# Eight dense projections of a two-layer block, joined into two chains of four with hand-placed buffers

## What is computed

```python
for layer in range(2):
    mod = (silu(c) @ ada_w[layer] + ada_b[layer])[:, None, :]
    sh1, sc1, g1, sh2, sc2, g2 = split(mod, 6)
    hh = rms_norm(x, norm1_g[layer]) * (1 + sc1) + sh1
    mix = nsa_mixer(hh, ...) if layer == 0 else rglru_mixer(hh, ...)
    x = x + g1 * mix                        # mix ends in @ w_out
    hh = rms_norm(x, norm2_g[layer]) * (1 + sc2) + sh2
    g, u = split(hh @ ffn_w_in[layer], 2)
    x = x + g2 * ((silu(g) * u) @ ffn_w_out[layer])
q, k, v = split(x @ w_qkv, 3)               # first step of the third layer
```

## The kernel before

| name | n, tiles, kt | matmuls | ahead of it | behind it |
|---|---|---|---|---|
| nsa_out | 4, 2, 8 | 192 | sparse attention | x mixed on VectorE |
| ffn0_in | 22, 2, 8 | 1056 | norm | h = silu(g)*u, split |
| ffn0_out | 8, 1, 22 | 528 | | x mixed |
| rg_in | 11, 2, 8 | 528 | norm | convolution, gelu |
| rg_out | 8, 1, 11 | 264 | recurrence | x mixed |
| ffn1_in | 22, 2, 8 | 1056 | norm | h, split |
| ffn1_out | 8, 1, 22 | 528 | | x mixed |
| da_in | 12, 2, 8 | 576 | x split | attention |

## Time and profile before

### The profile page before, as it was taken

How to read it: one execution, slowest core, us unless ns; L and a number is a source line. 1 busy time by engine, 2 the same in 40 slices (tenths; PEclk the granted TensorE clock), 3 DMA queues, 4 the chain that set the end, 5 groups by cost and what they waited for, 6 DMA issues and landing times. The chain is left out here.

```text
span 3203.3 us, 65861 instructions
## 1 busy us (share of the span) xinstructions
PE 2878.2 (90%) x27525; PEld 2113.0 (66%) x27525; DVE 1447.0 (45%) x2538; ACT 884.9 (28%) x1564; POOL 306.9 (10%) x422
## 2 busy tenths in 40 slices
PE   7999999999999999999989996874988899996985
PEld 5766778887856788888756763542567876663652
DVE  5678578533665433322374221212595654221222
ACT  3256332212454222213362000003342343000002
POOL 2125211001200000000000000001121430000001
PEclk9999999999999999999999998997899999998997
DMA  9720167442302333413217899997113217999997
GB/s 288 203 72 2 27 223 239 142 125 63 102 23 64 92 92 104 109 54 114 99 39 327 368 425 427 427 425 299 47 53 88 48 49 302 421 425 427 426 426 293
DMA packets 378757, 638.75 MB, mean 199 GB/s; under 512 B 91380, under 2 KB 328609, under 8 KB 344489
## 3 DMA queue, kind: packets, MB, share of 16 engines
q1 hardware_dynamic: 341497, 560.04, 47.8%
q0 software_dynamic: 15776, 51.63, 4.4%
q10 hardware_dynamic: 21264, 23.88, 2.2%
HBM read 611.06 MB, written 24.38 MB: 198 GB/s over the span
## 5 line engine op out<-in xcount | busy, mean ns | idle before, releaser
L2326 DVE TENSOR_TENSOR moe_scratch<-masks_b,moe_ps 128x128 f32<-128x128 f32 x102 | 39.4, 386 | 637.4 <-ACT masks_b L2183 637.4
L2125 PE MATMUL moe_ps<-moe_ring,moe_scratch 128*32 128x256 f32 x3616 | 233.1, 409 | 84.6 <-DMA moe_ring<-in_moe_w_gu 74.6
L217 PE MATMUL ffn_in_ps<-ffn_xhi,ffn_in_whi 128*128 128x512 f32 x704 | 274.8, 390 | 5.3 <-DVE ffn_xlo L493 4.4
L218 PE MATMUL ffn_in_ps<-ffn_xlo,ffn_in_whi 128*128 128x512 f32 x704 | 274.6, 390 | 0.0
L219 PE MATMUL ffn_in_ps<-ffn_xhi,ffn_in_wlo 128*128 128x512 f32 x704 | 274.5, 390 | 0.0
L2125 PEld LDWEIGHTS moe_ps<-moe_ring,moe_scratch 128*32 128x32 f32 x3616 | 137.4, 116 | 172.4 <-issue 90.3
L2110 PE MATMUL moe_ps<-xT,causal 128*32 128x256 f32 x3296 | 206.7, 389 | 0.0
L2110 PEld LDWEIGHTS moe_ps<-xT,causal 128*32 128x32 f32 x3296 | 127.8, 114 | 59.5 <-issue 10.8
L2183 ACT ACTIVATE masks_b<-moe_ps 128x128 f32<-128x128 f32 x102 | 28.4, 278 | 493.2 <-PE moe_ps L2125 491.2
L217 PEld LDWEIGHTS ffn_in_ps<-ffn_xhi,ffn_in_whi 128*128 128x128 f32 x704 | 132.6, 188 | 34.3 <-issue 5.4
L219 PEld LDWEIGHTS ffn_in_ps<-ffn_xhi,ffn_in_wlo 128*128 128x128 f32 x704 | 132.6, 188 | 27.4
(11 more groups left out here) (843 smaller groups left out, 6089.0 us busy)
## 6 DMA issues: line engine op xcount, KB each, us to landing
moe_ring<-in_moe_w_gu SPq DMA_DIRECT2D x80, 2048.0 KB, 37.7
moe_ring<-in_moe_w_down SPq DMA_DIRECT2D x40, 2048.0 KB, 35.0
da_moe_units<-in_moe_w_gu SPq DMA_DIRECT2D x24, 2048.0 KB, 37.9
rw_AR<-in_moe_w_gu SPq DMA_DIRECT2D x24, 2048.0 KB, 41.0
ffn_came<-in_ffn_w_in SPq DMA_DIRECT2D x88, 512.0 KB, 5.1
da_moe_units<-in_moe_w_down SPq DMA_DIRECT2D x12, 2048.0 KB, 32.5
rw_AR<-in_moe_w_down SPq DMA_DIRECT2D x12, 2048.0 KB, 29.9
ffn_late_lo<-in_ada_w POOLq DMA_DIRECT2D x32, 512.0 KB, 5.7
```

Of the source, the lines that this page charges most:

```text
L217: nc.tensor.matmul(ps[0:width, slot * tiles + o], high, xhi[:, k], start=(k == 0), stop=False)
L218: nc.tensor.matmul(ps[0:width, slot * tiles + o], high, xlo[:, k], start=False, stop=False)
L2125: last = nc.tensor.matmul(psGU[j * BLK:(j + 1) * BLK].rearrange("p (g a n) -> p g a n", g=2, a=2), xbT[:, k], cols[:, j], start=(k == 0), ...
L2326: V.tensor_tensor(h.rearrange("p (a m i) -> p a i m", a=2, m=2), gated.rearrange("p (a i m) -> p a i m", a=2, m=2), psU.rearrange("p (a i ...
```

## The change

The seven calls of `dense` from ffn0_in on and the one for nsa_out are replaced by eight `Dense` objects in two chains: nsa_out, ffn0_in, ffn0_out, rg_in, and rg_out, ffn1_in, ffn1_out, da_in. `run_chain` opens one block for a chain, and each engine runs through its four projections in order, held back by semaphores alone. All loops are written out. All buffers of a chain are put at byte addresses chosen by hand (`placed`), and its PSUM banks are shared (`ChainRoom`), so that the weights of the next projection have a place while the one before still runs.

- At the end of a projection ScalarE and VectorE split the first weight block of the next one (`after.first_high`, `after.first_low`) ahead of taking the last product. ffn_out splits 16 of 22 tiles then and the other six behind the last product. ffn1_in has its second block split ahead too (`second_before`).
- Where a norm follows, its squares are all made on ScalarE, two tiles of x in turn, in the projection ahead, and TensorE sums those of block i-2 ahead of the products of block i. ScalarE loads the table of the root (`warm_root`) there.
- The first block of a projection runs through kt in the outer loop. ffn_out starts when 19 of the 22 tiles of h are made, and waits for the last three singly. nsa_out gives its last block's two tiles to VectorE one by one. da_in splits its first tile of x ahead, the others behind.
- The fillers are (4, 5, 8) in place of (6, 3, 22) for ffn and (3, 3, 16) for rg_in; rg_out's three and da_in's six go, and so do those behind the last block of all but rg_in and da_in (12 and 3).
- `recycle` now runs ahead of nsa_out, between rg_in and the recurrence, and ahead of rg_out, and no longer ahead of ffn0_in and ffn1_in. The loads of ada_w may start when nsa_out's products are done, and `load_band` when ffn0_out's are.

```diff
+    def load(self, sp, i):
+        if i < 2 and self.preloaded[i]:
+            return
+        if i >= 2:
+            sp.wait_ge(self.low_done, self.split_at(i - 2))
+        elif self.before_load:
+            self.before_load(sp, i)
+        for dst, src in self.loads(self.first_raw if i == 0 else self.raw[i % 2], i):
+            sp.dma_start(dst, src).then_inc(self.w_loaded[i % 2], 16)
...
+    def products(self, pe, i):
+        nc = self.B.nc
+        if i == 0:
+            order = [(o, k) for k in range(self.kt) for o in range(self.tiles)]
+        else:
+            pe.wait_ge(self.low_done, self.split_at(i))
+            order = [(o, k) for o in range(self.tiles) for k in range(self.kt)]
...
+                if self.h_made is not None and o == 0 and (k == 0 or k >= self.kt - 3):
+                    pe.wait_ge(self.h_made, max(k + 1, self.kt - 3))
+            out = self.banks[i % 2][:, o]
+            nc.tensor.matmul(out, high, self.xhi[k], start=(k == 0), stop=False)
+            nc.tensor.matmul(out, high, self.xlo[k], start=False, stop=False)
+            last = nc.tensor.matmul(out, low, self.xhi[k], start=False, stop=(k == self.kt - 1))
...
+    def tensor(self, pe, after):
+        norm = after.norm if after else None
+        for i in range(self.n):
+            if norm and i >= 2:
+                norm.sum_tiles(pe, self.tiles_at(i - 2))
+            self.products(pe, i)
+            if self.parts and i == self.parts.fold_after:
+                self.parts.fold(pe)
+        if norm:
+            norm.sum_tiles(pe, self.tiles_at(self.n - 2))
+            stay_busy(self.B, self.unread, after.busy[0])
+            norm.sum_tiles(pe, self.tiles_at(self.n - 1))
+            stay_busy(self.B, self.unread, after.busy[1])
+            norm.spread(pe)
+            stay_busy(self.B, self.unread, after.busy[2])
+        if self.unread_behind:
+            stay_busy(self.B, self.unread, self.unread_behind)
...
+    def scalar(self, act, before, after):
+        norm = after.norm if after else None
+        if self.norm:
+            self.norm.root(act)
+            for k in range(self.kt):
+                self.norm.shift(act, k, self.xhi[k]).then_inc(self.x_hi_done, 1)
+        elif self.x is not None:
+            for k in range(1 if before else 0, self.kt):
+                self.x_high(act, k)
+        if before is None:
+            for q in range(len(self.first_parts)):
+                self.first_high(act, q)
+        for i in range(1, self.n):
+            if not (i == 1 and self.second_before):
+                self.split_high(act, i)
+            if self.act_body:
+                self.take_on_act(act, i - 1)
+            if norm and i >= 2:
+                norm.square_tiles(act, self.tiles_at(i - 2))
+        if after:
+            after.first_high(act, 0)
+            if after.x is not None:
+                after.x_high(act, 0)
+            if after.second_before:
+                after.split_high(act, 1)
+        if norm:
+            norm.square_tiles(act, self.tiles_at(self.n - 2))
+            norm.warm_root(act)
+        if self.act_body:
+            self.take_on_act(act, self.n - 1)
+        if norm:
+            norm.square_tiles(act, self.tiles_at(self.n - 1))
+        if after:
+            for q in range(1, len(after.first_parts)):
+                after.first_high(act, q)
...
+        elif self.x is not None:
+            for k in range(1 if before else 0, self.kt):
+                self.x_low(dve, k)
+        if self.dve_start:
+            self.dve_start(dve)
+        if before is None:
+            for q in range(len(self.first_parts)):
+                self.first_low(dve, q)
+        for i in range(1, self.n):
+            if not (i == 1 and self.second_before):
+                self.split_low(dve, i)
+            if self.parts:
+                self.parts.accumulate(dve, i)
+            if self.dve_body:
+                self.take_on_dve(dve, i - 1)
+        if after:
+            after.first_low(dve, 0)
+            if after.x is not None:
+                after.x_low(dve, 0)
+            if after.second_before:
+                after.split_low(dve, 1)
+        if norm:
+            norm.coefficients(dve)
+        if self.dve_body:
+            self.take_on_dve(dve, self.n - 1)
+        if after:
+            for q in range(1, len(after.first_parts)):
+                after.first_low(dve, q)
...
+    def square_tiles(self, act, tiles):
+        for k in tiles:
+            act.wait_ge(self.x_ready, k + 1)
+            if k >= 2:
+                act.wait_ge(self.summed, k - 1)
+            self.B.nc.scalar.activation(self.sq[:, k % 2], self.B.xT[:, k], self.B.ACT.Square).then_inc(self.squared, 1)
+    def warm_root(self, act):
+        self.B.nc.scalar.activation(self.spare, self.B.eps_rms[:], self.B.ACT.Sqrt)
+    def sum_tiles(self, pe, tiles):
+        for k in tiles:
+            pe.wait_ge(self.squared, k + 1)
+            sum_by_chunk(self.B, self.ps, self.sq[:, k % 2], k).then_inc(self.summed, 1)
...
-            dense(B, f"ffn{layer}_in", KF, 2, KD, P, P, loads, None, busy=(6, 3, 22), after=9, parts=parts, unrolled=parts is not None,
-                  act_body=lambda i, slot, ps: nc.scalar.activation(gated[:, slot], ps[:, 0], ACT.Silu),
-                  dve_body=product, xhi=xhi, xlo=xlo, norm=norm, sp_tail=early.load, slots=in_slots, coming=early)
...
+    first = Dense(B, N + "in", KF, 2, KD, loads, tiles_of(xhi, KD), tiles_of(xlo, KD), (came[:, 0], came[:, 1]), (whi[:, 0], whi[:, 1]), (wlo[:, 0], wlo[:, 1]),
+                  room.pairs, unread=room.unread, norm=norm, busy=(4, 5, 8), parts=parts, second_before=layer == 1,
+                  before_load=(lambda sp, i: sp.wait_ge(before.low_done, 2)) if layer == 1 else None,
+                  before_high=lambda act, i, q: act.wait_ge(before.products_done, before.n) if i == 1 and layer == 0 else None,
+                  before_parts=lambda pool: pool.wait_ge(before.products_done, before.n),
+                  act_body=lambda i, slot, ps: nc.scalar.activation(gated[:, slot], ps[:, 0], ACT.Silu), dve_body=product)
...
+    def out_load(sp, i):
+        if i == 0:
+            sp.wait_ge(first.low_done, first.split_at(KF - 1))
+        else:
+            sp.wait_ge(first.products_done, KF)
+    def out_high(act, i, q):
+        act.wait_ge(first.products_done, KF if i or q else KF - 1)
+    second = Dense(B, N + "out", KD, 1, KF, lambda w, i: [(w, w_out[:, :, i * P:(i + 1) * P])], tiles_of(hhi, KF), tiles_of(hlo, KF),
+                   (raw0[:], raw1[:]), (hi0[:], hi1[:]), (lo0[:], lo1[:]), room.singles, unread=room.unread, first_parts=[(0, 16), (16, KF)],
+                   h_made=h_made, before_load=out_load, before_high=out_high, dve_body=add_mixed(B, layer, 5, 1, x_done))
...
-        dense(B, "nsa_out", 4, 2, KD, P, P, out_loads, None, after=8, dve_body=add_mixed(B, 0, 2), xhi=ohi, xlo=olo, is_split=True, early=early, slots=(out_first[:], early.second[:]))
...
+    B.recycle(keep=[early.loaded, early.second_loaded, early.head_hi, early.head_lo])
+    mixed = [B.sem(f"x_mixed{q}") for q in range(2)]
+    chain_scope = ExitStack()
+    room = ChainRoom(B, "chain0", chain_scope)
+    first = Dense(B, "nsa_out", 4, 2, KD, out_loads, tiles_of(ohi, KD), tiles_of(olo, KD), (out_first[:], early.second[:]), (whi[:, 0], whi[:, 1]), (wlo[:, 0], wlo[:, 1]),
+                  room.pairs, unread=room.unread, early=early, dve_body=add_mixed(B, 0, 2, 2, mixed[0]), last_by_tile=True)
+    feed = ffn(B, 0, room, mixed[0], mixed[1], first)
+    return rg_lru(B, chain_scope, room, [first, *feed], mixed[1])
...
+        last = Dense(B, "rg_in", KR, 2, KD, in_loads, tiles_of(yhi, KD), tiles_of(ylo, KD), (in_came[:], in_second[:]), (high0[:], high1[:]), (low0[:], low1[:]),
+                     room.pairs, unread=room.unread, first_raw=in_first[:], norm=norm, busy=(4, 5, 8), unread_behind=12,
+                     before_load=lambda sp, i: sp.wait_ge(out0.products_done, out0.n) if i else sp.wait_ge(out0.low_done, 2),
+                     before_high=lambda act, i, q: act.wait_ge(out0.products_done, out0.n) if i else None,
+                     dve_start=pad, act_body=take, dve_body=convolve, pool_body=load_band)
+        run_chain(B, [*chain, last])
+        chain_scope.close()
+        B.recycle(keep=[tanhed, gelued, convolved, conv_chain, cubed])
...
+    last = Dense(B, "da_in", 12, 2, KD, qkv_loads(B), [x0[:, 0]] + tiles_of(xhi, KD - 1), [x0[:, 1]] + tiles_of(xlo, KD - 1), (w0[:], w1[:]), (high0[:], high1[:]),
+                 (low0[:], low1[:]), room.turned_pairs, unread=room.unread, first_raw=in_first[:], x=B.xT, x_ready=x_ready,
+                 before_load=lambda sp, i: sp.wait_ge(out1.products_done, out1.n) if i else sp.wait_ge(out1.low_done, 2),
+                 before_high=lambda act, i, q: act.wait_ge(out1.products_done, out1.n) if i else None,
```

(45 more changed lines are left out.)

369 lines of the change are left out of this document (251 added, 118 removed).

## The result

The changed kernel takes 3182.9 us (median of four runs, 3181.35 to 3185.16) where the kernel before took 3206.07 in the same session: a ratio of 0.9925, 95% interval 0.9913 to 0.9937. It is 23.2 us faster, and 3183 was forecast. The sum behind that number did not come out so well, as the traces show.

A forecast was written before the change was run, and what follows sets the result against it. TensorE, busy 90% of the span, was the bound, so only its lost time could go: of 62.1 us 38.5 stay, 23.6 less, span 3203.3 to 3179.7, median 3183 (own range 3177 to 3189; 8 in 10: 3173 to 3194).

The forecast's parts named there:

- The losses before: Joints, slow stretches and waits in the eight projections: 62.1 us lost, the most that the change could take away.
- The joint with a norm: Ahead of ffn0_in, rg_in and ffn1_in: 7.3 us still lost at each, 21.9 in all (bounds 6.8 and 9 each).
- The joints without one: Ahead of ffn0_out and ffn1_out 0.1 us each stays lost, 0.2; at da_in 0.5 (bounds 0.3 and 2).
- The sums that move: 16 tile sums between products of nsa_out, ffn0_out and rg_out: 0.35 us each, 5.6 (bounds 3.9 and 8).
- The second blocks: Waits for the second weight block: ffn0_in keeps its 0.9 us and rg_in gets one, 1.8 together.
- The barriers: Three new ones, ahead of nsa_out, the recurrence and rg_out, cost 5.1 us, covered by no work (bounds 3 and 6).
- The clock: Slow stretches at rg_out's start and the new barriers cost 3.4 us (bounds 0 and 7); none at the norms.
- Loops written out: Writing out the loops of five projections gains and costs nothing.
- the first: Clock falls at the norms all the same, and at new barriers: 16 to 19 us less, 3188 to 3191; chance 0.17.
- the second: Weight split ahead holds up the queue, five joints lose 2 to 3 us each: 3194 to 3198; chance 0.08.
- the fourth: TensorE starves for instructions in 50 newly written-out blocks: slower, 3233 at 1 us a block; chance 0.05.
- The third: More gained: sums hidden behind products, barriers covered, no slow stretch at all: 3171 to 3176; chance 0.09.

The follow-up runs named there:

- the weights behind the root: Changed kernel with first weight blocks of ffn0_in, rg_in and ffn1_in split behind root and reciprocal, ffn1_in's second block no longer ahead: ratio 0.9943 to the kernel before.
- the squares added: Changed kernel with squares of tiles 0 to 6 added up on VectorE, TensorE making two sums a norm, not eight: ratio 0.9913 to the kernel before.
- the written-out kernel: Kernel before with nsa_out, ffn0_out, rg_out, ffn1_in and ffn1_out written out in place of loops, nothing else: 3209.71 against 3208.66 us, ratio 1.0004.

## Why the prediction came out

The time and the direction are right; the sum for the eight projections is not. It said 23.6 us less for them, the traces show 19.5, and 4.8 us less behind them, with 1.6 us more ahead of them, made the total fit. The sum had no term for either, so that 3183 was met to a tenth is luck. Step by step:

- **The losses before**, 62.1 us: with the lengths in the table they are 62.0. The slow stretches took 1.6, 1.4 and 1.6 us from their blocks, not 1.7 each, and the two waits of 0.90 and 1.94 us are 1.06 and 2.1 from start to start. Where they fall differs between two profiles of the same kernel: the second of the kernel before has none behind rg_in's and rg_out's starts, but one behind ffn0_in's, at 422.4 us.
- **The joint with a norm**: 7.3 us each was forecast; 7.46, 7.26 and 7.27 are lost, 22.0 for the three (the first has two squares behind its last product). The chain from mixing to the first product came out of rows of the kernel before nearly to a tenth. The experiment with the weights behind the root shows that ending the split early is worth 1.7 us a joint, not the whole of the gain; the squares are worth more (2.7 us where the clock stays up, 4.9 where it falls). That experiment keeps the weights' load ahead. In the kernel before, the copy at rg_in also waited for the load:

```profile
791.10 1.06 ACT L252 ACTIVATE rg_in_whi<-rg_came 128x1024 fp32r<-128x1024 f32 x1 [2.18 <-DMA rg_came<-in_rg_w_in]
```

From the spread's start to the scaling's it was 4.50 us there; it is 3.00 with the split alone put back and 1.27 in the changed kernel. So at this joint another 1.5 us go with the late load, which no experiment takes out by itself.

- **The joints without one**: 0.0 in place of 0.1 at ffn_out, and da_in waits 0.25 us for its second x tile in place of 0.5. Right.
- **The sums that move**: the worst step. "I take 0.35 for each of 16: 5.6 us". It is 0.59 alone and 0.41 in a pair, by the blocks that shrink when they go: 12 x 0.59 + 4 x 0.41 = 8.7 us. I had priced them as a run of 64, with a little for the change of operands, and did not see that the change back is paid as well: in the rows above 0.32 us before the sum, 0.35 in it and 0.34 between the first two products behind it, where 0.227 is the pace.
- **The second blocks**: the wait stayed at ffn0_in and came at rg_in, as said, 0.9 us idle each and 1.06 from start to start.
- **The barriers**: "5.1 us" for three. The gaps that hold them grew by 1.42 (3.16 from the fillers to nsa_out's first product against 1.74), 1.27 and 0.84: 3.5 together. Only the second is tied to its barrier by an experiment; in the third, rg_out's fillers are gone too and TensorE waits 3.95 us for the split of its weights. I took the price from the one ahead of ffn0_in.
- **The clock**: "I take none" at the norms was right, and that it is the fillers that keep it so is shown by leaving them out: three slow stretches came, and the seven profiles of kernels that have the fillers, squares and split as the changed one has them, or the squares added, show none there. The Trainium skill (TensorE: Matmul & The Clock Gate, Part 1), by which only activity releases the throttled state, agrees. The length of one idle time doesn't decide: with the weights behind the root it was 2.55 us at all three norms, and one slow stretch came. "3.4" for the rest was too little. nsa_out lost 1.6 us and the recurrence 1.7 in slow stretches, and rg_out 2.8 in its 6.8 us (65.97 less 263 x 0.227 for products and 3.5 for sums): 6.1. That the barrier brings it is shown for the recurrence: a slow stretch stands at its start in all seven profiles with one ahead and in none of the three of new kernels without. At nsa_out it stands in eight of nine profiles with the barrier and four fillers, but the changed kernel without that barrier was not tried.
- **Loops written out**: nothing, now measured by itself.
- **Sum**: 22.0 + 8.7 + 0.3 + 2.1 + 3.5 + 6.1 = 42.7 stay of 62.0: 19.3 us less, against 19.6 and 19.4 read off the two pairs of profiles.
- "The loads of the experts and all that follows da_in only move": the profile shows 4.8 us less there and the second pair 7.0, beyond the 3 that I had named as making the forecast wrong. How long this part is goes with how long the clock is low in it; two profiles of the same kernel differ by up to 2 us in length and by 20 us in time at the lower level. Whether the change keeps the clock up there or whether two draws fell well stays open: the ratios, 0.9925 and 0.9927, mean 23 to 24 us, but their intervals reach down to 19.

Of the rivals, the first came half true, at the barriers and not at the norms; the second and the fourth are refuted, the second because at none of the joints with a split ahead did TensorE or the mixing wait for weights, the fourth by the written-out kernel. The third didn't come: the sums are paid in full, and the barriers are not covered.

## What to carry to other kernels

Read a joint from the timeline as a chain of instructions and price what is left behind the last product, then what moves: here the chain could be told to 0.2 us from the old rows. Work moved between the blocks of the engine that bounds the kernel isn't free, and a short operation of another kind costs it the switch both ways; let an idle engine add up first, which took another 8.6 us from the blocks here. Ahead of the recurrence a barrier cost its length (1.3 us) and 1.65 us of clock behind it, so where several projections are joined, the barriers that are left are the first place to look. And a forecast that is met has to be checked term by term: here the sum promised 4 us too much and a part outside it made up for that.

## What was not expected of the hardware

- Eight instructions of 128x128 that take 0.29 us in a run of 64 (2.28 us, waits included) cost 0.59 us between products of 128x512, and 0.41 for eight of 16.
- With the fillers gone TensorE idled at most 2.5 us at a time ahead of rg_in, and the clock went to 1.2 GHz for 6.8 us; with them there it idled 0.8 at most and stayed at 2.4 GHz through all three norms in both profiles of the changed kernel.
- With a barrier put in, the gap ahead of nsa_out grew by 1.4 us, of the recurrence by 1.3 and of rg_out by 0.8, the last with other edits in it.
